# Laying ring weights out panel by panel in a two-block decoder on one Trainium2 core

## What is computed

```python
D_MODEL, SEQ, D_FF, PEER_HEADS, PEER_TOPK = 1024, 256, 4096, 8, 16

def sq_relu_mlp(h, w_in, w_out):            # w_in 1024 x 4096, w_out 4096 x 1024
    return jnp.square(jax.nn.relu(h @ w_in)) @ w_out

# first block: attention, MLP 0, GLA, MLP 1
h = h + attention_mixer(hn, attn_w_qkv, ..., attn_w_o, rope)
h = h + gla_mixer(hn, gla_w_in, ..., gla_w_o)
h = h + sq_relu_mlp(rmsnorm(h, norm_mlp[i]), mlp_w_in[i], mlp_w_out[i])

# second block, for l in 0, 1
ada = c @ w_ada[l] + b_ada[l]               # 1024 x 6144 a layer: shifts, scales and gates
proj = h @ w_in[l]                          # 1024 x 5120
merged = sigmoid(gate_a) * (ya @ w_attn_proj[l]) + sigmoid(gate_c) * (yc @ w_conv_proj[l])
x = x + g1 * (merged @ w_out[l])
q = h @ w_query[l]                          # then scores, top 16 of each head, softmax
u, vv = expert_u[expert_idx], expert_v[expert_idx]
x = x + g2 * einsum(g * gelu(einsum(h, u)), vv)
```

## Time and profile before

| | us |
|---|---|
| runs shown (3) | 2376.71, 2380.03, 2380.29; median 2380.03 |
| profiled execution | 2375.75, span 2373.8 |
| TensorE, VectorE busy | 2107.6, 1604.4 |
| 0 to 880: first block and first mixer | TensorE 94 to 98% busy after the first 124 us, DMA 40 to 86% |
| 880 to 1480 and 1700 to 2374: expert layers | DMA engines full |
| 1480 to 1700: boundary and second mixer | TensorE 94%, DMA 58% |

### The profile page before, as it was taken

How to read it: one execution, slowest core, us unless ns; L and a number is a source line. 1 busy time by engine, 2 the same in 40 slices (tenths; PEclk the granted TensorE clock), 3 DMA queues, 4 the chain that set the end, 5 groups by cost and what they waited for, 6 DMA issues and landing times. The chain is left out here.

```text
span 2373.8 us, 24957 instructions
## 1 busy us (share of the span) xinstructions
PE 2107.6 (89%) x8857; PEld 1366.9 (58%) x8857; DVE 1604.4 (68%) x3325; ACT 804.7 (34%) x1746; POOL 569.6 (24%) x609
## 2 busy tenths in 40 slices
PE   8899999999999999998788778899999987887777
PEld 6688877789888765553333333597665543333333
DVE  7578855688966567765776675556586677667755
ACT  5545454554445422222122112355232211121222
POOL 0100010000002024334333333002133333333331
PEclk9999999999999999999989998999999999999999
DMA  7188934388854569999999999854499999999997
GB/s 287 47 310 304 340 124 146 125 336 326 322 193 144 178 262 417 421 421 421 421 421 421 421 420 422 338 183 166 168 415 421 421 421 421 422 421 421 421 422 308
DMA packets 161370, 772.80 MB, mean 326 GB/s; under 512 B 12999, under 2 KB 13383, under 8 KB 89582
## 3 DMA queue, kind: packets, MB, share of 16 engines
q0 software_dynamic: 80640, 587.24, 59.9%
q1 hardware_dynamic: 80622, 184.17, 21.8%
HBM read 770.27 MB, written 1.10 MB: 325 GB/s over the span
## 5 line engine op out<-in xcount | busy, mean ns | idle before, releaser
L2993 ACT ACTIVATE experts_diagonal<-ident,experts_weight 128x128 f32<-128x128 f32 x488 | 155.9, 390 | 638.8 <-DVE experts_weight L2870 627.7
L205 DVE TENSOR_TENSOR early_w_lo<-ring,early_w_hi 128x1024 fp32r<-128x1024 f32 x196 | 245.2, 1262 | 96.8 <-ACT early_w_hi L2272 53.5
L3136 PE MATMUL experts_fourth<-ring,experts_diagonal 128*128 128x512 f32 x464 | 222.5, 629 | 48.3 <-ACT experts_diagonal L2993 44.9
L2614 POOL DMA_INDIRECT ring<-in_experts_uv_dram,experts_at x196 | 188.4, 961 | 307.4 <-PE experts_fourth L3136 140.6
L2815 DVE CUSTOM_DVE_ANT_0 ring<-ring,experts_second 128x1024 f32<-128x1024 f32 x116 | 141.6, 1220 | 96.0 <-DMA ring<-in_experts_uv_dram,experts_at 95.3
L2614 POOL DMA_INDIRECT experts_v_slot<-in_experts_uv_dram,experts_at x160 | 155.3, 971 | 203.4 <-PE experts_fourth L3136 111.8
L3136 PEld LDWEIGHTS experts_fourth<-ring,experts_diagonal 128*128 128x128 f32 x464 | 90.8, 201 | 176.7 <-issue 104.3
L3136 PE MATMUL experts_fourth<-experts_v_slot,experts_diagonal 128*128 128x512 f32 x320 | 161.5, 647 | 32.3 <-ACT experts_diagonal L2993 32.1
L3136 PE MATMUL experts_first<-ring,experts_diagonal 128*128 128x512 f32 x320 | 157.0, 640 | 35.4 <-ACT experts_diagonal L2993 35.4
L3136 PE MATMUL experts_first<-experts_v_slot,experts_diagonal 128*128 128x512 f32 x320 | 147.3, 599 | 11.5 <-ACT experts_diagonal L2993 10.9
L210 PE MATMUL mlp_hid<-mix_hT_hi,early_w_hi 128*128 128x256 f32 x512 | 146.2, 286 | 4.0 <-DVE early_w_lo L205 2.0
(11 more groups left out here) (550 smaller groups left out, 4921.4 us busy)
## 6 DMA issues: line engine op xcount, KB each, us to landing
mlp_ada_rows<-in_ada_turned_dram POOLq DMA_DIRECT2D x48, 1024.0 KB, 8.4
ring<-in_w_in_dram SPq DMA_DIRECT2D x20, 2048.0 KB, 8.3
ring<-in_mlp_w_in_dram SPq DMA_DIRECT2D x16, 2048.0 KB, 11.7
ring<-in_mlp_w_out_dram SPq DMA_DIRECT2D x16, 2048.0 KB, 10.6
ring<-in_gla_w_in_dram SPq DMA_DIRECT2D x6, 2048.0 KB, 9.1
ring<-in_w_query_dram SPq DMA_DIRECT2D x6, 2048.0 KB, 8.6
ring<-in_w_out_dram SPq DMA_DIRECT2D x4, 2048.0 KB, 7.8
ring<-in_attn_w_qkv_dram SPq DMA_DIRECT2D x2, 2048.0 KB, 13.8
```

The source lines that it names most:

```text
L205: return dve.tensor_tensor(out_lo, a, hi.bitcast(F32), ALU.subtract)
L2614: pool.indirect_dma_start(pair(i), None, rows, bass.IndirectOffsetOnAxis(ap=at[:, n, j:j + 1], axis=0)).then_inc(pair_in[slot_of(i)], 16)
L2993: act.activation(diagonal[:, i % TOPK, :], K.ident[:], ACT.Copy, scale=weight[:, n, i % TOPK:i % TOPK + 1]).then_inc(diagonal_ready, 1)
L3136: mm = pe.matmul(y[n // PH][:, b, :], diagonal[:, j, :], v_row(i)[:, b * HALF:(b + 1) * HALF], start=n % PH == 0 and j == 0, stop=False, s ...
```

## The change

The host lays the ring's weights out anew before the launch: for each panel, partition p's 4096 floats stand in a row (16 KB), partition after partition, so that a panel is 2 MB in one piece. The views on the device follow. The 32 last columns of gla_w_in, which don't pass through the ring, become an array of their own, 1 KB a partition. The arrays hold the same numbers, and bytes moved, destinations, order and waits are as before. w_ada, the expert rows and the sub keys are not touched: they were rearranged on the host already.

```diff
 def columns(w, n):
-    return w[:, n * HALF:(n + 1) * HALF].rearrange("(k p) n -> p k n", p=P)
+    return w[n]
...
     def src_in(n):
-        return w_in.rearrange("(k p) n -> p k n", p=P)[:, :, bass.ds(n * HALF, HALF)]
+        return w_in[bass.ds(n, 1)].rearrange("a p k n -> (a p) k n")
 
     def src_out(n):
-        return w_out[bass.ds(n * HALF, HALF), :].rearrange("(k p) n -> p k n", p=P)
+        return w_out[bass.ds(n, 1)].rearrange("a p k n -> (a p) k n")
...
-        sp.dma_start(wz[:], A.gla_w_in[0][:, z0:z0 + 2 * RANK].rearrange("(k p) n -> p k n", p=P)
+        sp.dma_start(wz[:], A.gla_w_z[0]
                      ).then_inc(wz_ready, 16)
...
-    proj = [w[l].rearrange("(k p) n -> p k n", p=P) for w in (A.w_attn_proj_2, A.w_conv_proj_2)]
+    proj = [w[l, 0] for w in (A.w_attn_proj_2, A.w_conv_proj_2)]
...
+_BY_COLUMNS = ["attn_w_qkv", "attn_w_o", "gla_w_o", "mlp_w_in", "w_in_2", "w_out_2", "w_query_2"]
+_BY_ROWS = ["mlp_w_out", "w_attn_proj_2", "w_conv_proj_2"]
+
+def by_columns(w):
+    return np.ascontiguousarray(w.reshape(w.shape[0], -1, P, w.shape[2] // HALF, HALF).transpose(0, 3, 2, 1, 4))
+
+def by_rows(w):
+    return np.ascontiguousarray(w.reshape(w.shape[0], w.shape[1] // HALF, HALF // P, P, -1).transpose(0, 1, 3, 2, 4))
```

More of the change, by code:

```diff
@@ L1938, in pairs @@
                 for panel in ((columns(w_in, n), KC),
-                              (w_out[n * HALF:(n + 1) * HALF, :].rearrange("(k p) n -> p k n", p=P), 4))]
+                              (w_out[n], 4))]
     def conditions(layer):
@@ L2435, in experts @@
     out_panels, panels = take_panels(K, 2), take_panels(K, SLOTS)
-    queries = [(A.w_query_2[l][:, n * HALF:(n + 1) * HALF].rearrange("(k p) n -> p k n", p=P), KC) for n in (2, 3)]
+    queries = [(columns(A.w_query_2[l], n), KC) for n in (2, 3)]
     steps = [(c, t) for first in (0, PH) for t in range(T) for c in range(first, first + PH)]
@@ L3292, in program @@
         expert_layer(nc, K, A, memory, 1, out)
[L3295 to L3298, removed]
+_INS = ["x", "norm_mix", "norm_mlp", "attn_q_norm", "attn_k_norm", "gla_w_gate_up", "gla_b_gate", "gla_out_norm",
+        "final_norm", "c_2", "norm1_g_2", "norm2_g_2", "b_ada_2", "final_g_2"]
+_BY_COLUMNS = ["attn_w_qkv", "attn_w_o", "gla_w_o", "mlp_w_in", "w_in_2", "w_out_2", "w_query_2"]
[4 more added lines that the diff above has]
+    return np.ascontiguousarray(w.reshape(w.shape[0], w.shape[1] // HALF, HALF // P, P, -1).transpose(0, 1, 3, 2, 4))
 def rope_table():
@@ L3327 @@
     ins = {name: declare(name, _np.ascontiguousarray(inputs[name])) for name in _INS}
+    ins.update((name, declare(name, by_columns(_np.asarray(inputs[name])))) for name in _BY_COLUMNS)
+    ins.update((name, declare(name, by_rows(_np.asarray(inputs[name])))) for name in _BY_ROWS)
+    w = _np.asarray(inputs["gla_w_in"])
+    ins["gla_w_in"] = declare("gla_w_in", by_columns(w[:, :, :w.shape[2] // HALF * HALF]))
+    w = w[:, :, w.shape[2] // HALF * HALF:]
+    ins["gla_w_z"] = declare("gla_w_z", _np.ascontiguousarray(w.reshape(w.shape[0], -1, P, w.shape[2]).transpose(0, 2, 1, 3)))
     ins["experts_uv"] = declare("experts_uv", _np.stack([inputs["expert_u_2"], inputs["expert_v_2"]], axis=2))
```

## The result

The change made the kernel slower. Its median is 2387.77 us (2380.02 to 2396.31, 17 runs) against 2375.6 us for the kernel before on the same chip (17 runs): a ratio of 1.0053, with a 95% interval of 1.0043 to 1.0063, or 12.6 us of 2375.6 (the medians themselves lie 12.2 apart). I had forecast 2373.0 and a range up to 2382.0; both the sign and the range were wrong.

A forecast was written before the change was run, and what follows sets the result against it. DMA engines were taken to bound 1274 us, TensorE the rest. Gains of 4.4 (MLP waits), 0.6 (wait at 615.57) and 1.0 (expert layers) summed to 6.0 us; 2373.0 us was taken between 2372.2 and 2374.0, range 2367 to 2382.

The forecast's parts named there:

- What bounds the kernel, and who waits for what: Whole kernel: DMA engines bound 1274 us, TensorE the rest; one ada load's landing a turn sets five MLP waits, 4.92 us.
- I take 5.05 us (415 GB/s), the side of the 8 KB runs, since cost falls with the run's length.: Ring panels: 2.10 MB in 16 KB runs takes the engines 5.05 us, against 5.85 us in 2 KB runs.
- my sum: MLP turn: second panel runs from 158.4 to 163.5, 0.3 MB left at 162.7; ada load lands at 166.6, not 168.1.
- the slower rival: MLPs: panel pushes the ada load back if over 0.7 MB remains at its first data; 2384 to 2398 us, chance 0.1.
- The sharing: Panels beside gathers or ada loads: queues take turns by packet, so a 16 KB panel gets up to 280 GB/s, not some 90.
- With 16 KB packets the panel would take two thirds: Panel beside q0's 8 KB packets: two thirds of the engines' time, where 2 KB packets took 24%.
- 4.4 us gained: MLP loops: ada loads land earlier, so TensorE's waits for mlp_hidden_lo shrink; 4.4 us, bounds 2.5 and 4.9.
- 0.6 us at 615.57: TensorE's 2.01 us wait for early_w_lo: shrinks if the ada load lands 1.5 us earlier; 0.6 us gained, 0 to 1.0.
- 1.0 us in the expert layers: Both expert layers: engines move more while the query panel is mixed in with gathers; 1.0 us gained, 0 to 1.5.
- that rival: Start of an expert layer: gathers late by 2 to 6 us, cancelling the gain; 2376 to 2382 us, chance 0.05.
- The second rival: MLPs: the panel pushes the ada load back, landings at 10 us or more; 2384 to 2398 us, chance 0.1.
- some 17,400: Queue q1, whole kernel: packets expected after the change, 61 panels of 1024 and 20 of 512 packets becoming 128 each.

## Why the prediction was wrong

- **What bounds the kernel, and who waits for what: right in the main.** The longest of TensorE's MLP waits ends 2.75 us behind the landing of an ada load, as it was 2.76 before, and a turn is 45.28 us plus its waits as long as the clock holds. In the first turn of after two loads reach TensorE and not one (2.06 and 0.51 us).
- **The step that failed: "I take 5.05 us (415 GB/s), the side of the 8 KB runs, since cost falls with the run's length."** A 16 KB panel alone took 5.84 us. I had inferred a law of run lengths from the averages of two different queues, 359 and 413 GB/s. By the bound that I had written down myself (what 2 KB runs cost) the second panel of my sum, from 158.4, would have ended at 164.2, with 1.5 us or 0.55 MB left when the load's data came at 162.7, close to the 0.7 MB that I had named as the point from which the slower rival decides. My sum had also left out part of the ada load ahead: 151.3 + 2 x 5.85 + 2.5 is 165.5, with 1.0 MB left. The trace of after has it so. The load's first data came at 164.1, 3.8 us behind its issue as forecast; the panel had begun 1.7 us behind its issue and not 1.1. The queues of after at 160 to 164.1:

```profile
q1 hardware_dynamic: 64, 1.02, 78.4%
q0 software_dynamic: 63, 0.39, 23.0%
```

  So 0.39 MB of the load of 153.62 had moved in that time, and about 1.0 of its 2.1 MB were through. **1.1 MB were left, where my sum had 0.3.** The Trainium skill ("DMA: Bandwidth & Descriptors", Specifications) has full rate from 512 B up; I had weighed that against the trace and let the averages win. For a panel alone the rows of after agree with the skill: 58.4% against 58.5%.
- **The sharing: right in kind, applied to one load only.** "With 16 KB packets the panel would take two thirds" is what 67.2% and 33.9% show. But I worked out one load a turn and took the one ahead of it only as 2.5 us of work among the panels, whose own landing had no term. The load of 153.62 took 10.9 us. Its head met the w_out panel (at 157 to 159 it got 0.28 MB through, where before, beside 4 KB packets, 0.56 MB went in two microseconds), and its tail the next panel, at 9.2% of the engines. TensorE's wait of 2.06 us at 169.89 comes from it: DVE had waited for that load until 164.51. With "4.4 us gained" the term had the wrong sign: 8.6 us were lost.
- **0.6 us at 615.57: no.** The wait there is 2.01 us still (at 627.36). It isn't independent of the ada loads, for with these cut short it is 0.4 us or gone; but what its length hangs on no run shows.
- **1.0 us in the expert layers: about right, and too small to matter.** The query panel landed after 11.7 us, not the 5 or so that I gave it, but in the 30 us from its issue the engines moved 418 GB/s in both layers, against 405 and 407 before. Over all profiled executions the four kernels with query panels in 2 KB runs have 405 to 412 there, the thirteen in 16 KB runs 413 to 420. From that issue to the end of the kernel the second layer takes 659.7 to 661.2 us with the former (mean 660.7) and 658.9 to 660.2 with the latter (mean 659.6); for the first layer, up to the next panel of w_in, the means are 648.5 and 648.3. That is some 1.2 us for both layers, within the scatter of single executions. Equally, DVE waits for no gather between 1700 and 1760 of after: that rival fell.
- **The second rival came true.** "The panel pushes the ada load back", 2384 to 2398, with landings of 10 us or more as its sign: 10.3 to 11.4 us, and 2387.8. It had a chance of 0.1, on the argument that the panel is issued first in each turn. That holds for the load behind it (even so 1.1 MB of the panel were left), not for the load ahead of it, which is still under way when the panel comes.
- **Not foreseen: the clock.** The waits carried 1.5 us net on top.
- **The packets.** 17,774 came, where I wrote some 17,400; my own counts of panels give 18,286.

## What to carry to other kernels

Where two queues take turns by packet, the length of a contiguous run is the queue's weight against the others; a panel alone was hardly faster for it (5.94 to 5.86 us of the engines, 2 KB to 16 KB). So give short packets to the transfer that has slack and long ones to the one that is waited for. Before a layout is changed for longer runs, look for one transfer of each form alone in the trace, and list every transfer that is under way beside it, the one issued ahead of it too. And where the distance of pieces in HBM changes, measure a version with a little padding beside it; here that alone (1.0037 to 0.9979) was worth about as much as the size (1.0053 to 0.9988).

## What the runs showed of the hardware

- A 2 MB panel alone takes the engines 5.84 us in 16 KB runs and 5.85 us in 2 KB runs.
- Two queues that both have work moved equal or nearly equal counts of packets at every size looked at (16 KB: 35 and 35; 8 KB: 28 and 26; 4 KB: 66 and 68; 2 KB: 440 and 444; 1 KB: 47 and 46), so 16 KB against 8 KB is 67 to 34% of the time, 4 KB against 8 KB is 33 to 66%. The Trainium skill ("DMA: Bandwidth & Descriptors", Queues, rings and completion order) has this turn-taking, with a packet of some 9 to 17 descriptors; in these profiles one run of 1 to 16 KB was one packet, and the turns went by it.
- In the 30 us from the issue of a 2 MB query panel beside gathers the engines moved 405 to 412 GB/s with the panel in 2 KB runs (eight such stretches), 413 to 420 in 16 KB runs (26 stretches).
- 64 free bytes behind each 2 KB piece changed a panel's landing from 14.3 to 10.3 us (alone from 9.6 to 7.9) and the kernel from 1.0037 to 0.9979; 2 and 4 KB behind each piece made it 1.0115.
- The granted clock fell to 0.50 after idle times of TensorE of 3.52, 2.40 and 2.01 us, and stayed at 1.00 after others of 2.27, 2.06 and 2.01 us (at 619.46, 169.89 and 627.36 of after). Each fall cost about 1.6 us. The length of the idle time alone doesn't say whether it falls. The stretches behind the last three, in order of time:

```profile
170.00:172.00 2.00, 2.00 (x9) 1.66 (x10) 1.50 (x4) 1.47 (x2) 0.00 (x0) 1.00 0.90 258
...
621.00:623.00 2.00, 2.00 (x13) 1.77 (x12) 1.81 (x2) 0.00 (x0) 0.53 (x1) 1.00 0.78 311
627.00:629.00 2.00, 1.64 (x13) 1.65 (x14) 2.00 (x5) 1.07 (x2) 0.00 (x0) 1.00 0.69 291
```
